# Keys turned behind four exponentials, attention blocks turned in pieces between two banks

## What is computed

```python
def step(h, inp):                                  # scan over chunks of 128 tokens
    xc, dac, bc, cc = inp
    cum = jnp.cumsum(dac, axis=1)
    seg = cum[:, :, None, :] - cum[:, None, :, :]
    decay = jnp.exp(jnp.where(causal, seg, -jnp.inf))
    cb = jnp.einsum('bthn,bshn->btsh', cc, bc) * decay
    y = jnp.einsum('btsh,bshp->bthp', cb, xc)
    ...
def sparse_attend(q, ks, vs, valid):
    s = jnp.einsum('bthd,btkhd->bthk', q, ks).astype(jnp.float32) * HEAD_DIM ** -0.5
    s = jnp.where(valid[:, :, None, :], s, -jnp.inf)
    p = jax.nn.softmax(s, axis=-1).astype(vs.dtype)
    return jnp.einsum('bthk,btkhd->bthd', p, vs)
y_ssd = rms_norm(y_ssd.astype(x.dtype) * jax.nn.silu(z), params['ssd_norm_g'][l])
```

## Time and profile before

| | us |
|---|---|
| median of three runs | 3562.83 |
| lowest and highest run | 3554.72, 3569.42 |
| the profiled execution | 3555.62 |
| its span, first to last instruction | 3553.8 |
| PE busy | 3278.0 (92%) |
| DVE busy | 1903.4 (54%) |
| ACT busy | 1217.4 (34%) |
| POOL busy | 663.4 (19%) |
| mean granted TensorE clock | 0.942 |

### The profile page before, as it was taken

One profiled execution on the slowest core, in us unless ns is written; L12 is line 12 of the kernel. 1 busy time (PEld: TensorE's weight loads), 2 busy tenths in 40 slices (PEclk: granted clock), 3 DMA queues, 4 the chain that ended last, 5 costly groups with the idle time before them and its releaser, 6 DMA issues.

```text
span 3553.8 us, 49876 instructions
## 1 busy us (share of the span) xinstructions
PE 3278.0 (92%) x19418; PEld 2659.8 (75%) x19418; DVE 1903.4 (54%) x3006; ACT 1217.4 (34%) x2262; POOL 663.4 (19%) x663
## 2 busy tenths in 40 slices
PE   7899899877999999999999999997788999999997
PEld 4454466545989999999854544765478999999996
DVE  5579783333664434435454996733247544335345
ACT  3256714234242222212233666241434312212123
POOL 0000000011033333334200000001110433334331
PEclk9899999768999999999989999995789999999998
DMA  4111114216011111111111010341340111111111
GB/s 135 45 30 36 34 41 138 87 54 181 8 36 47 35 57 36 48 48 39 64 45 47 30 40 25 97 120 44 116 127 1 45 51 36 51 51 33 57 33 69
DMA packets 168248, 205.77 MB, mean 58 GB/s; under 512 B 61185, under 2 KB 136258, under 8 KB 166850
## 3 DMA queue, kind: packets, MB, share of 16 engines
q1 hardware_dynamic: 163394, 201.43, 18.9%
q10 hardware_dynamic: 4608, 1.05, 0.1%
HBM read 189.33 MB, written 13.08 MB: 57 GB/s over the span
## 4 chain that ended last, share of the span: by engine, by line
PE 69%; DVE 13%; issue 9%; ACT 6%; SPq 1%; DMA 1%; ACTq 0%; POOL 0%; DVEq 0%; POOLq 0%; PEldq 0%
PE PS L785 44%; PE PS L766 5%; DVE MIX L1748 4%; PE PS L798 2%; PE PS L867 2%; ACT X L1388 2%; PE PS L995 1%; PE PS L1168 1%; DVE WORK L1937 1%; SPq L445 1%; PE PS L1145 1%; PE PS L960 1%; PE PS L1155 1%; ACT WORK L1553 1%; PE PS L1183 1%
## 5 line engine op out<-in xcount | busy, mean ns | idle before, releaser
L785 PE MATMUL PS<-WORK_parts,WHIGH_parts 128*128 128x352 f32 x3936 | 806.8, 325 | 19.6 <-DVE MIX_parts L2249 11.2
L785 PEld LDWEIGHTS PS<-WORK_parts,WHIGH_parts 128*128 128x128 f32 x3936 | 669.3, 190 | 23.2 <-issue 23.2
L785 PE MATMUL PS<-WORK_parts,RING_parts 128*128 128x352 f32 x3024 | 655.8, 325 | 0.0
L766 PE MATMUL PS<-X,RING 128*128 128x512 f32 (+1 forms) x1824 | 602.3, 493 | 22.5 <-ACT MIX L1457 9.6
L766 PEld LDWEIGHTS PS<-X,RING 128*128 128x128 f32 x1824 | 303.8, 193 | 321.2 <-issue 319.1
L785 PEld LDWEIGHTS PS<-WORK_parts,RING_parts 128*128 128x128 f32 x3024 | 520.4, 189 | 0.0
L1748 DVE SCALAR_TENSOR_TENSOR WORK<-WORK,VEC 128x1072 f32<-128x1072 f32 (+1 forms) x236 | 483.7, 2050 | 8.4
L509 POOL TENSOR_TENSOR RING_parts<-RING,WHIGH_parts 128x1024 fp32r<-128x1024 f32 (+2 forms) x184 | 373.1, 2028 | 446.5 <-ACT WHIGH_parts L1337 442.0
L1337 ACT ACTIVATE WORK<-PS 128x32 f32<-128x32 f32 (+11 forms) x412 | 190.8, 514 | 732.4 <-PE PS L785 565.2
L785 PE MATMUL PS<-X_parts,WHIGH_parts 128*128 128x352 f32 x2016 | 436.1, 324 | 0.0
L1746 DVE TENSOR_SCALAR WORK<-WORK,VEC 128x1072 f32<-128x1072 f32 (+1 forms) x90 | 70.6, 784 | 515.5 <-ACT WORK L1337 515.5
(11 more groups left out here) (335 smaller groups left out, 4021.4 us busy)
## 6 DMA issues: line engine op xcount, KB each, us to landing
RING<-w_up SPq DMA_DIRECT2D x88, 512.0 KB, 3.5
RING<-cache_k SPq DMA_DIRECT2D x256, 128.0 KB, 2.2
RING<-cache_v SPq DMA_DIRECT2D x256, 128.0 KB, 2.2
RING<-w_in SPq DMA_DIRECT2D x46, 512.0 KB, 3.6
RING<-w_down SPq DMA_DIRECT2D x80, 256.0 KB, 2.6
RING<-cache_kidx SPq DMA_DIRECT2D x192, 32.0 KB, 1.7
WORK<-w_out SPq DMA_DIRECT2D x12, 512.0 KB, 6.3
MIX<-xT SPq DMA_DIRECT2D x3, 1408.0 KB, 9.8
```

The costliest lines, as they stand in the source:

```text
L766: mm = pe.matmul(job_psum(n, w, first=first), stationary(k), moving(k)[:, first:first + w], start=k == 0, stop=k == k_tiles - 1)
L785: mm = pe.matmul(thirds(n)[:, third, :], a, x[:, third * THIRD:(third + 1) * THIRD], start=k == 0 and part == 0, stop=k == tiles - 1 and p ...
```

## The change

In the scan stage a new semaphore, `near_decay`, is signalled by ACT's fourth exponential (head 3, the last that reads bank 2), and the first odd half group of a chunk waits for it in place of `decay`.

In the attention, a block is turned in pieces of up to four tiles, each into one bank, bank 4 for an even piece and bank 5 for an odd one (48 pieces). A piece waits for the copy of the piece two before it. PE's round becomes: pieces of block 2p-2, `scores(p)`, pieces of block 2p-1, steps set aside, `weigh(p-1)`. ACT copies the pieces of both blocks ahead of the exponentials of pair p. `take_out(i)` comes after the masks and reciprocals of block 4i + 7 on DVE, in place of after the mask of block 4i + 8. Since bank 5 is no longer free for it, the spreading is made in two calls: 10 matmuls in round 6 (first half and samples, banks 3 and 1) and 8 in round 7 (second half, bank 1), the latter after the first scaling. `scores(8)` now waits for both scalings.

```diff
+PIECES = [(_n, _s, min(_s + 4, BLOCKS[_n][0] + 1)) for _n in range(len(BLOCKS)) for _s in range(0, BLOCKS[_n][0] + 1, 4)]
+PIECES_OF = [[_q for _q, _piece in enumerate(PIECES) if _piece[0] == _n] for _n in range(len(BLOCKS))]
+PIECES_TO = [_of[-1] + 1 for _of in PIECES_OF]
...
                     if k % 8 == 1:
-                        pe.wait_ge(ssd["decay"], k // 8 + 1)
+                        pe.wait_ge(ssd["near_decay"], k // 8 + 1)
...
                     if p == NCHUNK:
-                        pe.wait_ge(rms["scaled"], 1)
+                        pe.wait_ge(rms["scaled"], 2)
...
-                def turn_block(n):
-                    i, h = BLOCKS[n]
-                    pe.wait_ge(att["normed"], n + 1)
-                    if n >= 1:
-                        pe.wait_ge(att["copied"], n)
-                    for s in range(i + 1):
-                        mm = pe.transpose(bank(4 + s // 4)[:, (s % 4) * P:(s % 4 + 1) * P],
-                                          SC[n % 4][:, s * P:(s + 1) * P], c("ident"))
+                def turn_piece(q):
+                    n, first, end = PIECES[q]
+                    if first == 0:
+                        pe.wait_ge(att["normed"], n + 1)
+                    if q >= 2:
+                        pe.wait_ge(att["copied"], q - 1)
+                    for key in range(first, end):
+                        mm = pe.transpose(bank(4 + q % 2)[:, (key - first) * P:(key - first + 1) * P],
+                                          SC[n % 4][:, key * P:(key + 1) * P], c("ident"))
                     mm.then_inc(att["turned"], 1)
...
-                    pe.wait_ge(att["copied"], 2 * p + 2)
+                    pe.wait_ge(att["copied"], PIECES_TO[2 * p + 1])
...
-                def spread_rstd():
-                    pe.wait_ge(rms["inverse"], 1)
-                    for ch, (first, L) in enumerate(CHUNKS):
-                        dst = bank((3, 5, 1)[ch // 4])[:, ch % 4 * P:ch % 4 * P + L]
+                def spread_rstd(again):
+                    if again:
+                        pe.wait_ge(rms["scaled"], 1)
+                    else:
+                        pe.wait_ge(rms["inverse"], 1)
+                    for ch in (4, 5, 6, 7) if again else (0, 1, 2, 3, NCHUNK):
+                        first, L = CHUNKS[ch]
+                        dst = bank(1 if ch >= NCHUNK // 2 else 3)[:, ch % 4 * P:ch % 4 * P + L]
...
-                    aside_steps = sample_steps(p)
+                    aside_steps = list(sample_steps(p))
+                    turned = 1 <= p <= n_pairs
+                    if turned:
+                        for q in PIECES_OF[2 * p - 2]:
+                            turn_piece(q)
                     if p < n_pairs:
                         scores(p)
-                    for now in list(aside_steps):
+                    if turned:
+                        for q in PIECES_OF[2 * p - 1]:
+                            turn_piece(q)
+                    for now in aside_steps:
                         now()
-                    if p == NCHUNK + 1:
-                        pe.wait_ge(rms["scaled"], 2)
+                    if p in (INVERTED_AT, INVERTED_AT + 1):
+                        spread_rstd(p > INVERTED_AT)
                     if 1 <= p <= n_pairs:
-                        turn_block(2 * p - 2)
-                        turn_block(2 * p - 1)
-                    if p == INVERTED_AT:
-                        spread_rstd()
-                    if p >= 2:
-                        weigh(p - 2)
+                        weigh(p - 1)
...
                     for h in range(SSD_HEADS):
-                        act.activation(DEC[rows, h, 0:L], bank(2 + h // 4, 512, rows)[:, (h % 4) * P:(h % 4) * P + L],
-                                       ACT.Exp, bias=NCUM[rows, ch, h:h + 1])
+                        ins = act.activation(DEC[rows, h, 0:L],
...
+                        if h == 3:
+                            ins.then_inc(ssd["near_decay"], 1)
...
-                    copy(PROBT[:, h, 0:keys], bank(4, keys)).then_inc(att["copied"], 1)
+                    copy(PROBT[:, BLOCKS[n][1], first * P:end * P], bank(4 + q % 2, (end - first) * P)).then_inc(att["copied"], 1)
...
                 for p in range(len(BLOCKS) // 2 + 1):
+                    if p >= 1:
+                        for q in PIECES_OF[2 * p - 2] + PIECES_OF[2 * p - 1]:
+                            copy_piece(q)
                     for n in (2 * p, 2 * p + 1):
                         if n < len(BLOCKS):
                             exp(n)
                     for m in turns_of_pair(p):
                         copy_sample(m)
-                    if p >= 1:
-                        copy_turned(2 * p - 2)
-                        copy_turned(2 * p - 1)
...
-                        dve.wait_ge(att["turned"], n - 3)
+                        dve.wait_ge(att["turned"], PIECES_TO[n - 4])
...
-                    dve.wait_ge(rms["spread"], 1)
+                    dve.wait_ge(rms["spread"], 2 if first == SEQ // 2 else 1)
...
-                    if n >= 8 and n % 4 == 0:
-                        take_out(n // 4 - 2)
-                for i in (NCHUNK - 2, NCHUNK - 1):
-                    take_out(i)
+                    if n >= 7 and n % 4 == 3:
+                        take_out(n // 4 - 1)
+                take_out(NCHUNK - 1)
```

More of the change, by code:

```diff
@@ L404, in build @@
             "keys_turned", "keys_copied", "keys_used", "fresh_keys_scored", "key_scores_kept"))
-        ssd = {n: sem("ssd_" + n) for n in ("da", "cum", "seg", "ws", "turned", "taken", "scores", "sums", "decay",
+        ssd = {n: sem("ssd_" + n) for n in ("da", "cum", "seg", "ws", "turned", "taken", "scores", "sums", "near_decay", "decay",
                                             "weighed", "y", "h", "state", "masked", "first_group")}
@@ L1552, in _ @@
                     for h in range(SSD_HEADS):
-                        act.activation(DEC[rows, h, 0:L], bank(2 + h // 4, 512, rows)[:, (h % 4) * P:(h % 4) * P + L],
-                                       ACT.Exp, bias=NCUM[rows, ch, h:h + 1])
+                        ins = act.activation(DEC[rows, h, 0:L],
+                                             bank(2 + h // 4, 512, rows)[:, (h % 4) * P:(h % 4) * P + L],
+                                             ACT.Exp, bias=NCUM[rows, ch, h:h + 1])
+                        if h == 3:
+                            ins.then_inc(ssd["near_decay"], 1)
                     act.activation(E2[:, :, 0:L], bank(4).rearrange("p (j t) -> p j t", t=P)[:, :, 0:L],
@@ L1567, in exp, with copy_piece @@
                                    accum_out=RSUM[:, n:n + 1]).then_inc(att["exp"], 1)
-                def copy_turned(n):
-                    i, h = BLOCKS[n]
-                    keys = (i + 1) * P
-                    act.wait_ge(att["turned"], n + 1)
-                    if n >= 4:
+                def copy_piece(q):
+                    n, first, end = PIECES[q]
+                    act.wait_ge(att["turned"], q + 1)
+                    if n >= 4 and first == 0:
                         act.wait_ge(att["out"], n // 2 - 1)
-                    copy(PROBT[:, h, 0:keys], bank(4, keys)).then_inc(att["copied"], 1)
+                    copy(PROBT[:, BLOCKS[n][1], first * P:end * P], bank(4 + q % 2, (end - first) * P)).then_inc(att["copied"], 1)
                 def exp_sample(m):
@@ L2220, in _ @@
                     elif n == 2 * INVERTED_AT + 1:
[L2221 to L2222 removed]
+                        scale_gated(SEQ, NS, bank(1, NS))
+                        scale_gated(0, SEQ // 2, bank(3)).then_inc(rms["scaled"], 1)
                     elif n == 2 * INVERTED_AT + 3:
[L2224 to L2228 removed]
+                        scale_gated(SEQ // 2, SEQ // 2, bank(1)).then_inc(rms["scaled"], 1)
+                    if n >= 7 and n % 4 == 3:
+                        take_out(n // 4 - 1)
+                take_out(NCHUNK - 1)
                 dve.wait_ge(smp["exp"], 2 * QUARTERS + QUADS)
```

7 lines of the change are left out of this document (2 added, 5 removed).

## The result

| us | before | after |
|---|---|---|
| median of the runs side by side | 3561.77 (4 runs) | 3512.80 (4 runs) |
| lowest and highest | 3554.72, 3569.42 | 3501.08, 3518.98 |
| the profiled execution | 3555.62 | 3501.08 |
| its span | 3553.8 | 3499.3 |
| PE busy | 3278.0 | 3243.4 |

The ratio of after to before is 0.9857, with a 95% interval of 0.9838 to 0.9877: 49 us less by the medians, 54.5 by the profiled executions. The forecast was 50.6 us less for the profiled execution and a median of 3507. In after the lines have moved by 5 to 15: the turning of keys is L1000 (was L995), scores L1150, turning of a piece L1161 (was L1155), weighing L1174, cached values L1227, spreading L1250, copies L1349 (was L1337), take_out L2180, scaling L2217, the wide exponential L1570 (was L1555), SyncE's page loads L450.

What follows compares the result with a forecast made beforehand. TensorE, busy 92% of the span, was taken as the bound, with its idle and low-clock time; SyncE's value pages come next. 2 x (7.2 + 18.1) = 50.6 off 3555.6 gives 3505.0, plus 2: 3507; range 3480 to 3540.

Steps and rivals of the forecast that it cites:

- Part 1: Scan stage: half key groups wait for the fourth exponential, not the wide one; 7.2 us gained a layer.
- The upper bound, 9.4: Scan stage: gain a layer if pages always decide, 8 x 1.17 us.
- Part 2: Attention up to the first value block: copy waits and spreading shrink; first value 5.3 us earlier, bounds 2 and 8.
- Part 3: Late attention pairs: value page stream sets the end, 79.9 us after first value; whole attention gains 18.1 a layer.
- 1 us for joints: Late attention: allowance beyond the value stream's pace, moving the stage's end from 848.3 to 849.3.
- so I count nothing for it beyond the 1 us below: Pair 7, late attention: some 10.3 us for 6.8, not counted because the value stream is later.
- if the pages don't hold 0.63 us each: Late attention: sign that the forecast is wrong, value pages not keeping 0.63 us each.
- The clock: Late attention, behind the first value: granted clock taken as 0.96 throughout, for 0.87 before; below 0.9 means wrong.
- Rival A: Late attention, pairs 11 to 15: the clock stays down; 3529, with the median's part 3531; chance 17%.
- Rival B: Attention before the values: higher clock, some 6 us a layer per tenth; 3483 at two tenths; chance 8%.
- Rival C: Late pairs: order on DVE makes the kernel slower, 13.8 us a pair against 11.5; 3587; chance 4%.
- Rival D: Late attention: waits only move, taking back what the copies gave; about 3544 in all; chance 7%.

Runs made afterwards that it cites:

- e7: After, with the scan's half group waiting for the eighth exponential in place of the fourth: 3525.07 us, ratio 0.9902 to before.
- e2: After, with the scan's wait put back on `decay`, so the attention's change alone: 3531.77 us, ratio 0.9948 to before.
- e3: After, with `take_out` right behind the masks of block 4i + 7, ahead of the reciprocals: 3505.70 us, ratio 0.9874 to before.
- e5: After, with half the columns of each value page from the fifth block on loaded, in as many transfers: 3511.41 us beside 3560.50 (one run).
- e6: After, with each value block from the fifth on loaded by one 512 KB transfer from four adjacent pages: 3497.40 us beside 3560.50 (one run).
- e10: e3, with the fourth page of each value block from the fifth on issued by ACT instead of SyncE: 3482.40 us, ratio 0.9802 to before.
- e11: e10, with both the third and the fourth page issued by ACT: 3493.96 us, ratio 0.9836 to before.
- e12: After itself, unchanged, run and profiled again on the chip of e10 and e11: 3507.91 us, ratio 0.9877 to before.
- e1: Before, with only the scan's half group waiting for the fourth exponential: 3530.14 us beside 3552.14, ratio 0.9942.
- e4: After, with ACT's copies behind the exponentials again while PE keeps its new order: 3567.77 us, ratio 1.0044 to before.

## Why the prediction was right, point by point

**Part 1, forecast 7.2 a layer, measured 11.3 and 11.4.** The mechanism is as predicted: L1000 is not released by L1570 any more, pages are waited for about as long (4.0, the longest 1.9), the next bound is the copy of the half group. In chunk 2 the next group is turned 0.65 earlier (forecast 0.75) and the loads start 1.36 earlier (1.17). The term was mis-sized in two ways. It counted the idle time, not the slower matmuls after it: PE's busy time in the stage fell by 8.0 us, with the clock from 0.88 to 0.92. The upper bound, 9.4, took the clock as given, and the measured value lies above it. And e7 shows that 0.69 us a chunk at this place cost 6 to 8 us a stage, not the 5.4 of its own waits. From one wide exponential to the next it is 14.8 to 16.8 us (in before 15.1 to 18.1), and 12.4 at the last (14.1); forecast were 15 to 16.

**Part 2, forecast 5.3, measured 7.1 and 5.2.** No copy wait of L1161 is left in pairs 1 to 6, and the spreading is 10 matmuls there. The difference between the layers is not the change: the nine kernels that share this order of PE, ACT and the samples' steps up to the first value (after, e2, e3, e5, e6, e7, e10, e11, e12) take 74.1 to 79.5 us in their 18 stages, 77.2 in the mean, at a clock between 0.54 and 0.60. Against before and e1, with 79.8 to 81.3 in four stages, the gain is some 4, with the 3.8 us of moved work already paid. The first value was forecast 76.0 us after the stage's start.

**Part 3, forecast 79.9 and 1 us for joints, measured 85.6 and 85.2.** The bound was named rightly (SyncE's pages), the waits that would show it too. The step that failed is pair 7, "so I count nothing for it beyond the 1 us below". Its timeline in after, from the first value on, which answers to the earlier trace rows:

```profile
752.81 1.49 PE L1227 MATMUL PS<-RING,WORK 128*16 128x256 f32 x24
...
754.23 1.16 PE L1250 MATMUL PS<-CONST,WORK 128*128 128x128 f32 x8
755.42 2.72 DVE L2217 SCALAR_TENSOR_TENSOR MIX<-MIX,VEC,PS 128x512 f32<-128x512 f32 x4 [1.29 <-PE PS L1250]
758.07 0.42 DVE L2180 COPY MIX<-PS 128x256 f32<-128x256 f32 x1
...
758.63 1.98 PE L1174 MATMUL PS<-WORK 128*64 128x128 f32 x16 [3.24 <-DVE MIX L2180]
...
761.58 1.56 PE L1150 MATMUL PS<-WORK 64*128 64x512 f32 x8
...
763.66 0.63 PE L1227 MATMUL PS<-RING,WORK 128*16 128x256 f32 x8
```

The chain is the predicted one (spreading, scaling, take_out, weighing), and from scores (748.77) to scores it takes 12.8 us for a forecast 10.3 (10.5 in layer 2). What was missed is what it does to the stream. SyncE's rows there:

```profile
753.68 7.61 SPq L450 DMA_DIRECT2D RING<-cache_v  x12
```

```profile
764.53 1.46 SPq L450 DMA_DIRECT2D RING<-cache_v  x3
```

The pair uses three blocks and so frees three slots, 12 pages, which are issued by 761.29; the next block is used at 763.66, and the next issue is at 764.53. For 3.2 us the engine that sets the pace has nothing to issue. "It falls on time when the value stream is the later one" treated the stream as running free, where it is fed by the very blocks that stand behind this pair. Layer 2 has a pause of the same length. The 112 issues took 79.0 us for 72.3. At that place 3.57 us lie from one issue to the next in place of 0.65, so 2.9 of these 6.7; the rest is in smaller pauses (e3, with 1.11 us at that place, still takes 76.8). A page took 0.71 us in the mean, which the prediction had named as a sign of being wrong ("if the pages don't hold 0.63 us each"). Against it the end was shorter than forecast, 5.7 us from the last issue for 6.7, and the 1 us for joints was in: 4.7 over in all.

Pairs from scores to scores were 5.4, 7.0, 8.9, 9.7, 7.6, 10.3 and 7.2 us for pairs 8 to 14; forecast 7.5 to 10, with the odd longer. The odd ones average 9.0, the even ones 7.3; but in layer 2 they are 6.3, 7.0, 10.5, 7.8, 7.4, 8.7 and 7.9, 7.8 for the odd and 8.0 for the even ones. That odd pairs are longer is not borne out.

**The clock** behind the first value was taken at 0.96 and is 0.93 and 0.94, up from 0.90 and 0.89. Rival A, that it stays down, is not the case, and in e10, with the same pieces going to and fro between banks 4 and 5, it is 1.00. The rule behind A (the Trainium skill, "TensorE: Matmul & The Clock Gate", section "A second HAM failure mode: psum-queue depth-cycling") therefore does not hold for these pieces by themselves.

What does lower the clock can only be read from the order of events. In the late part of before it falls at 808, 819, 829, 839 and 849 us, beside the ends of waits of 0.99, 2.27, 1.96, 2.65 and 2.31 us, so not only in "pairs with copy waits of 2 us and more". In e4, with seven waits of 3.3 to 4.3 us, it is 0.81. Yet the wait of after for a page at 780 us, the longest but one there, is followed by no fall: from 762.1 to 789.3 the clock is 1.00.

```profile
780.28 0.62 PE L1227 MATMUL PS<-RING,WORK 128*16 128x256 f32 x8 [3.07 <-DMA RING<-cache_v]
780.84 1.33 PE L1174 MATMUL PS<-WORK 128*64 128x128 f32 x20
```

So the length of one wait does not decide, and what does stays open.

**Rival B**, a faster first part, had 8%. In some executions it is there: 0.60 in layer 1 of after, where the part takes 74.2. It comes and goes between executions of one kernel (0.60 and 0.57 in after, 0.56 and 0.55 in e12), so it is nothing that the edit secures. Whether the edit makes it possible is open: the four stages of before and e1 have 0.54 or 0.55. **Rival C**, the DVE order, exists as a wait (6.7 us) and was worth 1.5 us a layer. **Rival D**, waits that only move, is half true. The late part of before had these waits:

```profile
PE PS L1155 <- ACT WORK L1337: 15.2, 10, 2.6
PE PS L1221 <- DMA RING<-cache_v: 5.6, 6, 1.6
```

With the last one for the closing vector work (1.7) that is 22.5 us; in after it is 18.2 (9.9, 6.7, 0.3, 0.2 and 1.1). So about 70% of the 14.9 us of copy waits that went came back, as waits for pages and take_out. The 4.3 us that did not, and 3.9 less of busy time (69.6 to 65.8, with 12 matmuls fewer in this part), make its 8.1.

**The median.** The medians of before and after stand 6.2 and 11.7 us above their profiled executions; I had allowed 2 for after (7.2 for before). The profiled run of after (3501.1, its lowest) is 3.9 under its forecast of 3505.0; the allowance was 9.7 too small, and so the median is 5.8 over 3507.

## What to carry to other kernels

When a stage is fed by a stream through a few slots, count the instructions that issue it as the work of an engine: here 0.65 us for each page made SyncE the bound, and moving one issue in four to ScalarE's queue brought more in that part of the stage (14.1 and 12.7 us) than the change had (8.1 and 8.2). Do not cancel a longer pair against a stream that is late, as long as the pair itself frees the slots. And price an idle time of TensorE of about a microsecond at more than its length, if in the trace before slower matmuls follow it.

## What the runs showed that I had not expected

- Half the bytes of the value pages changed the late part by 1.1 and 0.1 us, a quarter of the issues by 7.3 and 6.9. So the one transfer of 512 KB in place of four of 128 KB did not hold anything up.
- Up to the first value block the changed kernel ran at a granted clock of 0.60 in one execution and 0.55 in another, 74.2 against 79.4 us (layer 1 of after, layer 2 of e12; layer 1 of e12 took 77.6). This alone can move a profiled execution by 3 to 5 us a layer, as much as the whole term of part 2.
- With the page issues shared, the late attention had a clock of 1.00 while PE was still idle for 8.7 of 69.8 us, in gaps of up to 1.3 us (1.5 in layer 2). ScalarE's issue of a page takes 0.35 us in its queue's rows and cost the exponentials and copies nothing visible at one a block, but with two a block the copies were late by up to 2.2.
